# A sparse mixer split by token tile: tile 1's attention between expert slices

## The reference

```
h = h + nsa_mixer(rms_norm(h, l0_attn_norm), ...)     # sparse mixer
h = h + peer_ffn (rms_norm(h, l0_ffn_norm), ...)      # experts, layer 0
h = h + fox_mixer(rms_norm(h, l1_attn_norm), ...)     # forgetting attention
h = h + peer_ffn (rms_norm(h, l1_ffn_norm), ...)      # experts, layer 1
return rms_norm(h, final_norm)
```

## Time and profile before

| what | value |
|---|---|
| median of three runs | 2725.19 us (2722.46 to 2730.38) |
| the profiled execution | 2720.3 us, of which the span is 2718.5 us |
| busy in the span | PE 2223.6, DVE 1422.1, POOL 1163.9, ACT 848.8 us |
| moved by DMA | 750.54 MB, 544.02 MB of them in POOL's gathers |
| first gather of experts | at 1081.7 us |
| the four folds | at 1491.0, 1912.7, 2340.1 and 2709.9 us |

### The profile page before, as it was taken

How to read it: one execution, slowest core, us unless ns; L and a number is a source line. 1 busy time by engine, 2 the same in 40 slices (tenths; PEclk the granted TensorE clock), 3 DMA queues, 4 the chain that set the end, 5 groups by cost and what they waited for, 6 DMA issues and landing times.

```text
span 2718.5 us, 26748 instructions
## 1 busy us (share of the span) xinstructions
PE 2223.6 (82%) x8440; PEld 1387.4 (51%) x8440; DVE 1422.1 (52%) x2909; ACT 848.8 (31%) x2079; POOL 1163.9 (43%) x1115
## 2 busy tenths in 40 slices
PE   5879999789988768767877798887799888767776
PEld 4657877668856557324522454363465354222322
DVE  2364445454455344883844655456565447664443
ACT  2434434444422342221222224212225213222221
POOL 0000000000000100775777666757676757777774
PEclk8899999899988989888988899898899889888888
DMA  7414544135534104999999899999899999989997
GB/s 225 176 40 161 185 159 165 62 139 185 185 118 176 63 1 179 408 333 373 386 366 367 343 416 367 399 393 384 334 412 384 380 368 328 376 312 372 368 369 286
DMA packets 165294, 750.54 MB, mean 276 GB/s; under 512 B 18289, under 2 KB 18433, under 8 KB 152513
## 3 DMA queue, kind: packets, MB, share of 16 engines
q0 software_dynamic: 149168, 544.02, 53.1%
q1 hardware_dynamic: 13664, 192.94, 18.9%
q10 hardware_dynamic: 2352, 12.24, 1.2%
HBM read 744.94 MB, written 4.19 MB: 276 GB/s over the span
## 4 chain that ended last, share of the span: by engine, by line
PE 23%; POOL 14%; issue 9%; DMA 7%; DVE 5%; another core or an unknown queue 1%; ACT 0%; DVEq 0%; ACTq 0%; POOLq 0%
PE ps L849 14%; POOL Z L1907 14%; DMA Z<-v,experts 7%; PE ps L864 6%; DVE Z L1645 3%; PE ps L871 2%; DMA Z<-u,experts 1%; PE ps L892 0%; PE ps L902 0%; DVE xn L1668 0%; DVE o L1660 0%; DVE ranks L1573 0%; PE ps L951 0%; PE ps L903 0%
## 5 line engine op out<-in xcount | busy, mean ns | idle before, releaser
L849 PE MATMUL ps<-Z 128*128 128x512 f32 x2048 | 1015.8, 653 | 271.0 <-DMA Z<-v,experts 203.2
L849 PEld LDWEIGHTS ps<-Z 128*128 128x128 f32 x2048 | 416.8, 209 | 840.2 <-issue 560.6
L1645 DVE CUSTOM_DVE_ANT_0 Z<-Z,xn 128x1024 f32<-128x1024 f32 x512 | 610.4, 1224 | 346.0 <-DMA Z<-u,experts 274.6
L1907 POOL DMA_INDIRECT Z<-u,experts x512 | 558.2, 1090 | 309.4 <-issue 154.0
L1907 POOL DMA_INDIRECT Z<-v,experts x512 | 570.5, 1114 | 273.5 <-PE ps L849 128.4
L1466 DVE TENSOR_TENSOR ring_lo<-ring,ring_hi 128x1024 fp32r<-128x1024 f32 x220 | 255.4, 1220 | 278.1 <-ACT ring_hi L1029 278.1
L592 PE MATMUL ps<-ring_hi,xT_lo 128*128 128x512 f32 x624 | 251.6, 403 | 34.9 <-DVE xT_lo L1514 20.7
L1029 ACT CAST ring_hi<-ring 128x1024 fp32r<-128x1024 f32 x220 | 214.8, 1050 | 152.8 <-DMA ring<-panels 136.8
L593 PE MATMUL ps<-ring_lo,xT 128*128 128x512 f32 x624 | 245.7, 394 | 0.0
L594 PE MATMUL ps<-ring_hi,xT 128*128 128x512 f32 x624 | 245.5, 393 | 0.0
L864 PE MATMUL ps<-o,ring 128*128 128x128 f32 x1536 | 197.6, 288 | 50.9 <-issue 48.8
(11 more groups left out here) (244 smaller groups left out, 2058.0 us busy)
## 6 DMA issues: line engine op xcount, KB each, us to landing
ring<-panels SPq DMA_DIRECT2D x91, 2048.0 KB
Z<-u,experts POOLq DMA_INDIRECT x512
Z<-v,experts POOLq DMA_INDIRECT x512
gain<-gains ACTq DMA_DIRECT2D x4, 1024.0 KB, 8.0
pj<-keys ACTq DMA_DIRECT2D x4, 1024.0 KB, 7.9
bias_lines<-xn POOLq DMA_DIRECT2D x1, 3072.0 KB, 37.5
gain<-gains ACTq DMA_DIRECT2D x5, 512.0 KB, 4.8
Z<-bias_lines POOLq DMA_DIRECT2D x1, 2048.0 KB, 9.8
```

Of the source, the lines that this page charges most:

```text
L849: last = mm(ps[:, c, :], diag[s], vrow[s][:, c * NC:(c + 1) * NC], start=slot == 0, stop=slot == SLOTS - 1)
L1645: v.tensor_tensor_reduce(out=urow[s], in0=urow[s], in1=xn[:, t, :], scale=1.0, scalar=0.0, op0=ALU.mult, op1=ALU.add, accum_out=hdot[:, t, ...
L1907: g.indirect_dma_start(out=rows[s], out_offset=None, in_=tables[layer], in_offset=bass.IndirectOffsetOnAxis(ap=experts[:, t, slot:slot + 1 ...
```

## The change

The sparse mixer leaves the list of steps after "nsa", with its barriers and its fillers, and becomes two stages of the other scheme.

- `middle`, before the first tick and before `route00`: the compression of all tokens (T, H, G, C), the compressed attention of both tiles (c, !m, !x, !n, X, e), the turning of queries and keys (A, B, D, E), and for tile 0 alone the eight batches (two sources x four groups, four heads each: S, P, O), the output projection (o, u) and the norm.
- `nsa1`, in window 0, ticks 6 to 18: tile 1's eight batches, output projection (with the two output panels loaded a second time) and norm. `route01` moves from ticks 10 to 15 to ticks 20 to 26 and its choices from 18 and 39 to 28 and 41. `route00` ranks its last heads at ticks 2 to 6 and chooses at tick 7 (before 3 to 8, and 9).
- POOL copies keys twice over (`twin`), in 8 copies, and keeps tile 1's values in another place (`kept_v`), all ahead of the first gather.
- Turned projections (w, q, k) become `project_late` and four transposes of the result (W, Q, K, in `turn_projected`) in all windows, with one ACT copy more each.
- The compression and output panels are used unsplit, as float32.
- The gain rows "fox" and "ffn1" are loaded in window 0, as their place holds tile 1's keys until then.

```diff
+MIDDLE = [["A0", "A1", "T0", "T1"],
+          ["T2", "T3", "D0", "E0"],
+          ["H0", "S0a", "S0b", "!E0"],
+          ["H1", "S1a", "S1b", "P0a", "!E1", "B0", "B1"],
+          ["H2", "G0", "G1", "S2a", "S2b", "P1a", "O0", "!E2", "C0"],
+          ["H3", "S3a", "S3b", "P2a", "O1", "!E3"],
+          ["G2", "c0", "c1", "S4a", "S4b", "P3a", "O2", "!m", "!E4", "!x", "G3"],
+          ["S5a", "S5b", "P4a", "O3", "!n", "!E5", "C1"],
+          ["S6a", "S6b", "P5a", "O4", "!E6", "X0"],
+          ["S7a", "S7b", "P6a", "O5", "!E7", "e0", "e1"],
+          ["P7a", "O6", "D1", "E1"],
+          ["O7", "e2", "e3"],
+          ["o0", "o1"], ["u0", "u1"]]
+def nsa_plan(t):
+    for i in range(NSA_BATCHES + 2):
+        names = in_batch("S", t, i) if i < NSA_BATCHES else []
+        names = names + ([f"O{i - 2}"] if i >= 2 else [])
+        names = names + (in_batch("P", t, i - 1) if 1 <= i <= NSA_BATCHES else [])
+        plan.append((6 + i, names))
+    return plan + [(16, ["o0", "o1"]), (17, ["u0"]), (18, ["u1"])]
...
-STAGES = [("route00", -1, [(0, ["y0", "y1", "w0", "s0", "w1", "w2", "s1", "w3", "s2", "s3"])]),
-          ("route01", 0, [(k - 8, names) for k, names in LATE_ROUTE]),
+STAGES = [("middle", -20, list(enumerate(MIDDLE))),
+          ("route00", -1, [(0, ["y0", "y1", "w0", "W0", "s0", "w1", "w2", "W1", "s1", "w3", "W2", "s2", "W3", "s3"])]),
+          ("nsa1", 0, nsa_plan(1)), ("route01", 2, LATE_ROUTE),
...
-            def project_turned(key):
-                w, to = late_panel(key), bank(key)
+            def turn_projected(key, blocks):
+                emptied(pe, (key[0], key[1].lower()))
+                to = bank(key)
                 for j in range(4):
-                    for k in range(KT):
-                        last = mm(to[:, j * P:(j + 1) * P], w[:, k * NC + j * P:k * NC + (j + 1) * P], tokT[:, k, :],
-                                  start=k == 0, stop=k == KT - 1)
+                    last = tr(to[:, j * P:(j + 1) * P], blocks[:, j, :], ident)
                 last.then_inc(bank_filled, 1)
...
+            def add_batch(key):
+                filled(dve, key)
+                v.reciprocal(share[:, :], totals[i % 2][:, :])
+                v.tensor_tensor(share[:, :], share[:, :], gates[:, t, gate_at:gate_at + BATCH], ALU.mult)
+                for j in range(BATCH):
+                    last = v.scalar_tensor_tensor(out=acc[:, own], in0=shadow_bank(key)[:, own], scalar=share[:, j:j + 1],
+                                                  in1=acc[:, own], op0=ALU.mult, op1=ALU.add)
```

More of the change, by code:

```diff
@@ L663, in scores @@
                         own = slice(m * HD, (m + 1) * HD)
[L665 to L669, removed]
+                        q, k = qkT[u][own, 0:SEQ], qkT[u][own, SEQ + CW:]
+                        last = mm(ps[:, 2 + m, 0:P], q[:, 0:P], k[:, 0:P], start=True, stop=True)
+                        last = mm(ps[:, 2 + m, P:P + SEQ], q[:, P:SEQ], k, start=True, stop=True)
                     last.then_inc(s_done, 1)
@@ new lines, in nsa_out, with turn_four @@
+            def nsa_out(key):
+                t = block_of(key)[0]
+                if key[1][0] == "o":
+                    emptied(pe, (key[0], f"O{NSA_BATCHES - 1}"))
+                    turn_half(key, gathered_mix[t])
+                else:
+                    emptied(pe, (key[0], "o1"))
+                    project_late(key)
+            def turn_four(key, sources):
+                to = bank(key)
+                for j, a in enumerate(sources):
+                    last = tr(to[:, j * P:(j + 1) * P], a, ident)
+                last.then_inc(bank_filled, 1)
@@ L896, in fox_scores, with nsa @@
+            def nsa(stage, begin, plan):
+                for tick, names in plan:
+                    yield begin + tick
+                    for name in names:
+                        (nsa_out if name[0] in "ou" else nsa_batch)((stage, name))
             def fox_scores(key, t):
@@ L962, in beside @@
                 for stage, begin, plan in STAGES:
-                    if stage[:3] == "fox":
+                    if stage == "middle":
+                        yield from middle(stage, begin, plan)
+                    elif stage == "nsa1":
+                        yield from nsa(stage, begin, plan)
+                    elif stage[:3] == "fox":
                         yield from fox(stage, int(stage[3]), begin, plan)
@@ new lines, in nsa @@
+            def nsa(stage, begin, plan):
+                for tick, names in plan:
+                    yield begin + tick + 1
+                    for name in names:
+                        key, kind, i = (stage, name), name[0], int(name[1])
+                        if kind == "o":
+                            copy_bank(key, tokT[:, 4 * i:4 * i + 4, :], fours(key))
+                            if i == 0:
+                                load_late_gain("fox")
+                                load_late_gain("ffn1")
+                        elif kind == "P":
+                            copy_shares(key)
+                        elif kind == "S" and name == in_batch("S", 1, i)[-1]:
+                            soft_exps(stage, i)
+                root()
@@ new lines, in nsa @@
+            def nsa(stage, begin, plan):
+                for tick, names in plan:
+                    yield begin + tick + 1
+                    for name in names:
+                        if name[0] == "S":
+                            soften((stage, name))
+                        elif name[0] == "O":
+                            add_batch((stage, name))
+                        elif name[0] == "u":
+                            add_out((stage, name))
+                dve.drain()
+                norm_late(1, "ffn0", xn_ready)
```

688 lines of the change are left out of this document (403 added, 285 removed).

## The result

The kernel after takes 2595.81 us (median of four runs, 2586.78 to 2606.08), the kernel before 2723.82 us in the runs beside it: a ratio of 0.9544, 95% interval 0.9475 to 0.9612. The profiled execution has a span of 2601.2 us, 117.3 less than the one of before.

The account below looks back on a forecast made before the run. The expert stream sets the end once begun, so all work ahead of the first gather, bound by hand-overs and barriers, is on the path. 2720.3 - 97 + 12 - 2 = 2633; forecast 2636 us, range 2604 to 2682.

Parts of the forecast that it names:

- The front: Ahead of the first gather: the shorter middle stage brings that gather from 1081.7 to 984.5, -97 us (bounds -50 to -113).
- Rival 1: Middle stage bound by latency, not PE: first gather near 1025, total 2673 us; chance 0.17.
- Windows 1 and 2: Expert windows 1 and 2: fewer instructions in the turned projections gain 2 us (bounds +5 to -25).
- rival 3: More is won: instruction fetch held windows 1 and 2, and window 0's bytes fit its gaps; 2603 us, chance 0.12.
- Window 0: First expert window: tile 1's added work fits beside the stream, its extra bytes cost +12 us (bounds +0 to +45).
- The sum: Whole kernel: the profiled 2720.3 us with the terms -97, +12 and -2 gives 2633 us.
- Rival 2: Window 0: gathers are held for all of DVE's added work, 45 us, total 2678 us; chance 0.08.
- Rival 4: Window 0: in-order engines lock step and the ring of 8 rows runs dry; 2725 to 2740 us, chance 0.03.

Follow-up runs that it names:

- half_compression: The kernel after with 8 of the 16 contraction steps in each compression product; 2515.97 us against 2530.29 on the quick chip.
- before_late: The kernel before with only its turned projections (w, q, k) made 16 records of 512 columns and four transposes; quick chip, 2602.64 us, ratio 1.0004.
- after_d: The kernel after unchanged, run as the measure on the quick chip; 2530.29 us, ratio 0.9715 to the kernel before.
- neither: The kernel after without tile 1's eight attention batches and its output projection with two panels; 2506.31 us against 2530.29 on the quick chip.
- after_again: The kernel after once more, unchanged, on the quick chip; 2530.36 us, ratio 0.9715 to the kernel before.
- before_late_b: The kernel before with only its turned projections made 16 records and four transposes, on a slow chip; 2687.07 us, ratio 0.984.
- after_c: The kernel after unchanged, as the measure on a slow chip; 2609.83 us, ratio 0.9559 to the kernel before.
- after_more: The kernel after unchanged, profiled on a slow chip; 2596.03 us, ratio 0.9549 to the kernel before.
- after_turned: The kernel after with the turned projections of the kernel before, on the quick chip; 2524.86 us, ratio 0.9689 to 0.9716 to the kernel before.
- after_turned_b: The kernel after with the turned projections of the kernel before, on a slow chip; 2642.46 us.
- after_split_b: The kernel after with w, q and k projected in four column groups, 64 records a panel for 16, turns kept; slow chip, 2666.58 us.

## Why the prediction was wrong, step by step

**The front (forecast -97): right.** First gather at 979.9 for a forecast 984.5, and at 974 to 983 in the fourteen other profiles of the kernel after and its variants with whole compression. PE is busy 90% till the norm, and half_compression shows PE as the bound. Rival 1 (latency) falls. Two errors of the sum cancel here: PE was busy 93.5 us and not 83.4 (granted clock 0.83 in that stretch), and stood idle for 10 us and not for the 20 that 956 - 852.6 leaves.

**Windows 1 and 2 (forecast -2, bounds +5 to -25): this step failed.** I had the row, 32.6 us of "issue" in front of the turned projections, and wrote that most of it lies beside DMA that is saturated anyway. It does not: the two windows were 37 us shorter in the first pair of profiles and 39 in the second, and on chips of this kind the projections are worth 42 us in the kernel before and 33 in the kernel after, for idle times of 43 to 52 us over all of their panels. So most of the idle time was on the path. The term also left out window 0, whose second routing has four such panels; in before, 18 of the 50.9 us lie outside windows 1 and 2. The profile's page gave a hint that the earlier trace rows left out: its chain by line has "PE ps L864 6%". Saturation was read from the DMA share of 0.97, but the same windows moved 390 and 384 GB/s afterwards for 381 and 370 before. A mean share of 0.97 says nothing on whether 10 us of late records on PE starve the ring of 8 rows; POOL's wait for PE does (85.6 us in those windows in the trace of before, 36.0 after). This is the first half of rival 3, which had a chance of 0.12 and a price of 2603, 7 us from the time; its sign came true too ("issue" waits of these panels 0.5 for 32.6 us, windows 16 and 21 us shorter). That the price came so near is luck: its +4 for window 0 (bytes that fit the gaps) was 30, and its -18 for windows 1 and 2 was -37, with 8 more in window 3.

**Window 0 (forecast +12, bounds 0 to +45): the mechanism was incomplete and the term too small.** With the projections equal on both sides, on the quick chip (before_late and after_d), it costs 409.24 - 379.38 = 29.9 us. I had weighed 11 us of PE work a tick against a mean tick of 12.8 us. But that mean holds the stops; a free tick takes 10.2 us (8 gathers of 0.524 MB at the 410 GB/s of the later stretch above), and PE with a batch needs 10.75 at least, and 14 with a panel, which is over even the mean of 12.8. So PE takes over as the bound while tile 1 runs, as the 351 GB/s show, beside the bytes. Of the 29.9 us, 20.6 are the batches and the projection, as window 0 of neither shows; the other 9 (the gain rows' 1 MB, by estimate 2.6 us at 400 GB/s, among them) were not taken apart. The bound had held it.

In the first pair of profiles the table by windows is blurred too: the kernel after issues 275 gathers in window 0 for 265, since POOL was further ahead at the fold. Ten gathers are 5.2 MB, 14 us of the 30, and are missing in the windows behind. So only the sum of the windows is a clean number, -15 us there.

**The sum.** In the first pair of profiles the four terms were forecast -97, +12, -2 and 0 (window 3) and measured -102, +30, -37 and -8. Without the projections the change is worth 72 us on the quick chip (before_late to after_again) and 77 on a slow one (before_late_b to after_c), for 85 forecast (-97 + 12). With them it is worth 119.5 us on that slow chip, for 87 in the sum: the projections brought 40 us more than forecast and the rest 8 less. On the quick chip, where the change is worth 73 us, the forecast of 89 is 16 us too good. In the first timing and on the chip of after_more the difference is 128 and 130 us; the further 10 were not taken apart.

**The others.** A gather beside an expert dot does take longer: in the trace of before, between 1500 and 1900 us, 111 gathers that overlap a dot took 1.29 us on the mean and the 135 others 0.96. The added DVE work did not add to that. Rival 2 (gathers held by DVE's added work) falls: POOL is busy 303.25 us for 275 gathers in window 0, 1.10 us each, as before (292.22 for 265). Rival 4 (lock step) falls: on the quick chip the ticks with batches take 10.75 to 17 us, and in the first profile five ticks took 80.

**Still open.** For what the instructions are late. The DMA queues of the kernel before and after (kind, packets, MB, share) are
```profile
q8 instruction: 54, 0.88, 0.1%
```
and
```profile
q8 instruction: 48, 0.79, 0.1%
```
16 KB a packet, fewer with fewer instructions: with the old projections the kernel after has 56 (after_turned, 0.92 MB), and the kernel before with the new ones 46. Those 8 packets (0.13 MB) come with 1056 more records on PE and as many weight loads, 62 bytes each by estimate. The Trainium skill, page Advanced Engine Details and Errata, section "Sequencer and Instruction Queues", says that an engine's instructions are cached in lines of 16 KB, which are 256 instructions; the packet's size (0.88 MB in 54) agrees. So do the 62 bytes, as 16 KB by 256 are 64.

The traces do show where the late instructions are. PE's waits for "issue", all lines together, are 1 to 5 us ahead of the first gather in every profile, on the quick chip and the slow ones. Beside the stream they are 38 to 106 us on the slow chips and 3 to 10 on the quick one. So they come beside the stream of gathers on a slow chip, and they do not end with the old projections: in windows 1 and 2 on the chip of after_c they sum to 34.0 (before_late_b) and 37.0 (after_c) with the new ones, 47.2 (after_turned_b) and 65.7 (after_split_b) with 64 records a panel. That a line of instructions comes late beside the gathers would fit this and the single records of after_turned_b, but no run here changed the loading of instructions alone, so it is argued, not shown.

## What to carry over

Idle time in front of late instructions is a real price where that engine's next item frees a buffer of the stream: cost it in full as one bound of the range, whatever the DMA share says, and halve it only with a reason. Compare added work in a tick with the shortest tick of the trace, not with the mean, which already holds the stops. Split a change by undoing its parts on more than one chip before the gain is put down to a part, and compare streams by the sum of their windows.

## What the runs showed of the hardware

Chips differ by as much as this change brings: the kernel before takes 2603 us on one (in both timings there) and 2724 to 2730 on four timings elsewhere. The part ahead of the stream is equal to 4 us (first gather 1081.7 to 1085.7), and the unchanged window 3 has 334 to 344 us on the one and 355 to 370 on the others. What makes the one chip quicker was not looked for. Records of 0.11 us on PE can come 1.4 to 2.8 us apart for part of a panel on the slow chips, and did not on the quick one. Fewer, longer instructions bought 33 to 42 us on a slow chip at equal PE work.
